# Score units and row turns placed between the v row tiles, small first-layer loads issued later: a two-layer diffusion and mixture-of-experts step

## The reference, cut to what matters

```python
def token_mixer(u, p, lam_init, rope, ctx_kv):
    proj = u @ p['w_in']
    a_in, q, k, v, c_in = jnp.split(proj, [o1, o2, o3, o4], axis=-1)
    y_pool = multiscale_pool(a_in, p['pool_w'], p['pool_scale'])
    ...
    q = apply_rope(q, cos, sin)
    k_att = jnp.concatenate([apply_rope(k, cos, sin), ctx_kv[0]], axis=1)   # latent tokens
    v_att = jnp.concatenate([v, ctx_kv[1]], axis=1)
    o = diff_attention(q, k_att, v_att, lam)       # softmax(q1 k1) - lam * softmax(q2 k2), 4 heads
    y_conv = conformer_conv(c_in, ...)             # GLU, 31 taps, LayerNorm, SiLU, pointwise
    y = jnp.concatenate([y_pool, y_attn, y_conv], axis=-1) @ p['w_out']
    return y, k, v
def trunk_layer(x, mod, p, lam_init, rope, ctx_kv):
    u = x * (1 + scale1) + shift1                  # mod = SiLU(cond) @ w_mod + b_mod
    y, k, v = token_mixer(u, p, lam_init, rope, ctx_kv)
    x = layer_norm(ALPHA * x + gate1 * y, ...)
    u = x * (1 + scale2) + shift2
    return layer_norm(ALPHA * x + gate2 * hier_moe(u, p), ...), k, v
```

## Time and profile before

| | us |
|---|---|
| median of 3 runs (1090.07 to 1093.93) | 1090.11 |
| the profiled execution | 1091.42 |
| its span in the trace | 1089.8 |
| TensorE busy with matmuls in the span | 927.5 (85%) |
| VectorE / ScalarE / POOL busy | 371.2 / 237.4 / 178.4 |

### The profile page before, as it was taken

One profiled execution on the slowest core, in us unless ns is written; L12 is line 12 of the kernel. 1 busy time (PEld: TensorE's weight loads), 2 busy tenths in 40 slices (PEclk: granted clock), 3 DMA queues, 4 the chain that ended last, 5 costly groups with the idle time before them and its releaser, 6 DMA issues.

```text
span 1089.8 us, 14815 instructions
## 1 busy us (share of the span) xinstructions
PE 927.5 (85%) x5692; PEld 551.3 (51%) x5692; DVE 371.2 (34%) x915; ACT 237.4 (22%) x568; POOL 178.4 (16%) x214
## 2 busy tenths in 40 slices
PE   5999899974999876888889998998488887778886
PEld 3655465533555534454545645553355554445444
DVE  0178452255111111112527846224611111111135
ACT  2110365042111110121220026603311111012113
POOL 5000000003222222221020000000322222222200
PEclk9999999996999999999999998999699999989998
DMA  9992261295999999997995216309699999899951
GB/s 305 373 386 115 95 251 61 87 371 203 383 413 415 413 413 413 412 392 311 380 369 215 116 46 236 125 21 376 247 354 412 414 414 413 345 415 410 414 223 58
DMA packets 80900, 321.93 MB, mean 295 GB/s; under 512 B 13359, under 2 KB 25991, under 8 KB 57537
## 3 DMA queue, kind: packets, MB, share of 16 engines
q1 hardware_dynamic: 66016, 295.72, 68.7%
q0 software_dynamic: 14816, 25.29, 6.4%
HBM read 321.46 MB, written 23.59 MB: 317 GB/s over the span
## 4 chain that ended last, share of the span: by engine, by line
PE 67%; DMA 13%; DVE 7%; SPq 6%; ACT 5%; issue 2%; POOLq 0%; ACTq 0%; DVEq 0%; POOL 0%
PE ps L1169 15%; PE ps L910 11%; DMA ring<-in_w_up 8%; PE ps L1184 8%; PE ps L1122 8%; PE ps L913 4%; PE ps L885 3%; PE ps L841 2%; DMA arena<-u_rows,row_idx 2%; PE ps L1177 2%; SPq L611 2%; SPq L604 2%; DMA ring<-in_w_mod 2%; ACT arena L1435 1%; DMA y_pairs<-tail,row_idx 1%
## 5 line engine op out<-in xcount | busy, mean ns | idle before, releaser
L1169 PE MATMUL ps<-ring,tail 128*64 128x256 f32 x1760 | 205.1, 384 | 10.2 <-DMA ring<-in_w_up 8.4
L1169 PEld LDWEIGHTS ps<-ring,tail 128*64 128x64 f32 x1760 | 144.2, 139 | 83.1 <-issue 25.2
L1908 DVE TENSOR_TENSOR arena<-arena,ps 128x128 f32<-128x128 f32 x68 | 19.5, 287 | 365.3 <-ACT arena L1470 365.3
L910 PE MATMUL ps<-uT,ring 128*128 128x384 f32 x352 | 118.2, 493 | 2.0 <-ACT uT L1319 2.0
L1184 PE MATMUL ps<-ring,krow 128*64 128x512 f32 x408 | 104.8, 633 | 3.0 <-issue 2.2
L738 POOL DMA_INDIRECT y_pairs<-tail,row_idx x58 | 57.7, 994 | 289.5 <-ACT tail L1495 283.6
L910 PEld LDWEIGHTS ps<-uT,ring 128*128 128x128 f32 x352 | 67.4, 192 | 46.2 <-issue 3.4
L1495 ACT ACTIVATE tail<-ps 128x512 f32<-128x512 f32 x58 | 34.6, 597 | 190.3 <-PE ps L1184 190.3
L733 POOL DMA_INDIRECT arena<-u_rows,row_idx x66 | 68.9, 1043 | 36.3 <-issue 20.1
L1625 DVE SCALAR_TENSOR_TENSOR arena<-arena,dw 128x414 f32<-128x414 f32 x118 | 67.6, 644 | 0.0
L1470 ACT ACTIVATE arena<-ps 128x128 f32<-128x128 f32 x68 | 18.9, 278 | 214.0 <-PE ps L1169 197.2
(11 more groups left out here) (281 smaller groups left out, 1059.8 us busy)
## 6 DMA issues: line engine op xcount, KB each, us to landing
ring<-in_w_gate SPq DMA_DIRECT2D x55, 1024.0 KB, 17.9
ring<-in_w_up SPq DMA_DIRECT2D x55, 1024.0 KB, 23.8
ring<-in_w_down SPq DMA_DIRECT2D x55, 1024.0 KB, 23.5
ring<-in_w_mod SPq DMA_DIRECT2D x10, 3072.0 KB, 10.8
arena<-in_w_gate SPq DMA_DIRECT2D x13, 1024.0 KB, 16.1
arena<-in_w_up SPq DMA_DIRECT2D x13, 1024.0 KB, 19.8
arena<-in_w_down SPq DMA_DIRECT2D x13, 1024.0 KB, 19.3
ring<-in_w_in SPq DMA_DIRECT2D x8, 1536.0 KB, 17.1
```

The lines of the kernel that those rows point to most:

```text
L910: last = mm(ps[:, n % 4, 0:T], slot[s][:, k, c:c + P], uT[:, k, :], start=(k == 0), stop=(k == KD - 1))
L1169: last = mm(ps[W * half:W * (half + 1), b, 0:2 * P].rearrange("p (j f) -> p j f", j=2), xc[:, b, k, :], gate_up_w[s][:, :, k, half * P:(ha ...
```

## The change

In layer 0, POOL waits until the fourth of the first modulation products is done before it issues the 11 small loads. On TensorE, in both layers, the key turns go between v tiles 0 and 1; the convolution turns and the scores of units 0 and 1 go between v tiles 1 and 2. For that the key turns use banks 0 and 1, and the third v tile uses bank 5. ScalarE's program follows the same order: the first v eviction, the two key copies, the second v eviction, the root, the exponentials of units 0 and 1, the third v eviction. Since `uT` is still read by the third v tile when the convolution rows are normalized, `crow` moves into the convolution accumulator and the squares' scratch `sq_out` into the GLU buffer.

```diff
-        sq_out = cacc.rearrange("p c n -> p (c n)")[:, 0:6 * VD].rearrange("p (b n) -> p b n", b=6)
+        sq_out = csil.rearrange("p c n -> p (c n)")[:, 0:6 * VD].rearrange("p (b n) -> p b n", b=6)
...
-        crow = uflat[:, 2 * T + NT * AW:2 * T + NT * AW + NT * CONV].rearrange("p (t n) -> p t n", t=NT)
+        crow = cacc.rearrange("p c n -> p (c n)")[:, 0:NT * CONV].rearrange("p (t n) -> p t n", t=NT)
...
                 pool.dma_start(dw_rows[0:TAPS, :], g["conv_dw"][l:l + 1].rearrange("o k n -> (o k) n")).then_inc(taps_loaded.sem, 16)
+                if l == 0:
+                    pool.wait_ge(mod_rows.sem, FIRST)
+                    pool.nop(nofuse=True)
                 pool.dma_start(ck_rows, g["cache_k"][0, l:l + 1].rearrange("o t h m d -> (o t) (h m d)")).then_inc(mix_loaded.sem, 16)
...
                 def project(n, s, c, rows=None, sig=proj_ready):
 
-                    if n >= 4:
+                    bank = 5 if n == 16 else n % 4
+                    if n == 16:
+                        wait(roped, l, 8)
+                    elif n >= 4:
...
-                for t in range(NT):
+                def rows_out(t):
+
                     project(14 + t, 2, 2 * P, rows=t, sig=slot_done[2] if t == NT - 1 else proj_ready)
-                    if t == 0:
-                        rotate(7)
-
-
-                wait(proj_act, l, 13)
+
+                rows_out(0)
+                rotate(7)
+                wait(proj_act, l, 12)
                 wait(mix_loaded, l, 7)
                 for h in range(HEADS):
-                    last = tr(ps[:, 2, h * P:(h + 1) * P], ck_rows[:, h * P:(h + 1) * P], ident)
+                    last = tr(ps[:, 0, h * P:(h + 1) * P], ck_rows[:, h * P:(h + 1) * P], ident)
                 last.then_inc(ck_turned.sem, 1)
-                wait(proj_act, l, 14)
                 for h in range(HEADS):
-                    last = tr(ps[:, 3, h * P:(h + 1) * P], kT[:, h, 0:SEQ], ident)
+                    last = tr(ps[:, 1, h * P:(h + 1) * P], kT[:, h, 0:SEQ], ident)
                 last.then_inc(ck_turned.sem, 1)
+                rows_out(1)
 
                 wait(conv_done, l, 1)
...
-                wait(ck_copied, l, 2)
-                wait(roped, l, 8)
...
+                wait(ck_copied, l, 2)
+                wait(roped, l, 8)
+                scores(0)
+                wait(proj_act, l, 14)
+                scores(1)
+                rows_out(2)
                 wait(proj_act, l, 15)
...
-                for u in range(NU + 3):
+                for u in range(2, NU + 3):
...
-                for t in range(NT):
+
+                def take_rows(t):
+
                     proj_wait(14 + t)
-                    fn(vrow[:, t, :], ps[:, (14 + t) % 4, 0:AW], ID).then_inc(proj_act.sem, 1)
+                    fn(vrow[:, t, :], ps[:, (2, 3, 5)[t], 0:AW], ID).then_inc(proj_act.sem, 1)
+
+                take_rows(0)
                 wait(ck_turned, l, 1)
-                fn(ckT, ps[:, 2, :].rearrange("p (h t) -> p h t", h=HEADS), ID).then_inc(ck_copied.sem, 1)
+                fn(ckT, ps[:, 0, :].rearrange("p (h t) -> p h t", h=HEADS), ID).then_inc(ck_copied.sem, 1)
                 wait(ck_turned, l, 2)
-                fn(krow[:], ps[:, 3, :], ID).then_inc(ck_copied.sem, 1)
+                fn(krow[:], ps[:, 1, :], ID).then_inc(ck_copied.sem, 1)
+                take_rows(1)
                 wait(cln_var, l, 1)
...
                         last.then_inc(scores_used.sem, 1)
+                    if u == 1:
+                        take_rows(2)
                     if u >= 3:
```

More of the change, by code:

```diff
@@ L909, in project @@
                         if rows is None:
-                            last = mm(ps[:, n % 4, 0:T], slot[s][:, k, c:c + P], uT[:, k, :],
+                            last = mm(ps[:, bank, 0:T], slot[s][:, k, c:c + P], uT[:, k, :],
                                       start=(k == 0), stop=(k == KD - 1))
                         else:
-                            last = mm(ps[:, n % 4, 0:AW], uT[:, k, rows * P:(rows + 1) * P], slot[s][:, k, c:c + AW],
+                            last = mm(ps[:, bank, 0:AW], uT[:, k, rows * P:(rows + 1) * P], slot[s][:, k, c:c + AW],
                                       start=(k == 0), stop=(k == KD - 1))
```

## The result

| | median, us | ratio to before, 95% interval |
|---|---|---|
| before (6 runs, 1090.07 to 1093.93) | 1091.15 | |
| changed (6 runs, 1080.82 to 1086.29) | 1084.51 | 0.9928 [0.9911, 0.9945] |

The change makes the kernel faster by 0.55 to 0.89%, clear of the half per cent; the medians alone differ by 6.64 us, 0.61%. One run in each of two later sets, at a far lower clock (1431.6 and 1641.83 us), is left out of the ratios. The profiled execution took 1084.30 us with a span of 1082.6, 7.2 us under that of before. Lines after the change are renumbered: L888 is the old L885, L868 the old L865, L919 the old L913, L994 the old L992, L1004 the old L1002, L844 the old L841, L1377 the old L1367. In the experiments they shift once more by a few lines; the tiles and shapes in the rows tell them apart.

A forecast was written before the change was run, and what follows sets the result against it. TensorE was taken as the bound, two thirds of the chain, DMA waits second. Terms 2.0 + 1.8 + 1.8 = 5.6 us (7.3 or 9.0 with clock held in one or both layers) off 1090.11 gave 1082.4, range 1079.5 to 1087.0.

The forecast's parts named there:

- The start: Layer 0 start: later small loads let the second modulation slice land sooner; gain 2.0 us, bounds 0 to 2.0.
- The clock: Attention's start, each layer: 1.7 us gained where full clock holds, bounds 1.0 to 2.0; leaned to at least one layer.
- rival 1: Attention's start: clock falls in both layers as before, no clock gain; 1084.5 us, chance 0.25.
- TensorE can use only the 2.01 us that it waits: Second modulation product at the start: slice up to 3.5 us sooner, but gain capped by TensorE's wait, taken 2.0.
- The price of 0 for the moved loads: q and k columns of w_in: moved loads share DMA engines, landing unchanged near 58 to 59; priced 0, range 0 to 2.
- The order: Projections to attention: turns and scores moved between v tiles bring unit 2's scores and second turn 1.8 us sooner per layer.
- The named successor of the wait: Ahead of the second turn: VectorE's maximum of unit 2, then probabilities, leave some 1.7 us idle instead of 1.15.
- half clock reaching into the modulation products: Attention's modulation products: listed as a sign that the prediction was wrong; no size given.
- rival 2: Start: gives nothing, as the second slice is late for its own length or w_in lands late; 1086.5 us, chance 0.10.
- rival 3: Projections to attention: new order gives little, through third eviction, changes of work or experts' streaming; about 1087.5 us, chance 0.13.
- rival 4: Start: slower, as moved loads hold up w_in; at 12 us late about 1096 us, chance 0.05.
- I pass the whole sum on: Later stages, experts' weight streaming included: start from TensorE signals that move up alike, so the whole sum reaches the end.

The follow-up runs named there:

- experiment 2: Changed kernel with the small loads issued as early as before, so the new order alone; ratio to before 0.9958, median 1087.86 us.
- experiment 7: Changed kernel with only the four router loads issued later, the other seven small loads as early as before; one run, 1081.71 us.
- experiment 4: Changed kernel plus unread products in TensorE's two idle stretches of each layer; ratio to before 0.9897, median 1080.48 us.
- experiment 3: Changed kernel with VectorE making unit 1's probabilities ahead of its maximum of unit 2; ratio to before 0.9891, median 1079.5 us.
- experiment 1: Kernel before with only the small loads issued later, old order of work; ratio to before 0.9964, median 1088.17 us.
- experiment 8: Kernel before, old order, plus unread products in TensorE's two idle stretches at attention's start; ratio to before 0.9984, median 1090.59 us.
- experiment 6: experiment 5 with modulation product parts in attention put two units earlier; ratio to before 0.9846, median 1075.1 us.
- experiment 5: experiment 3 with the third v eviction's wait moved from ahead of unit 2's scores to the second turn; ratio to before 0.9900, median 1081.39 us.

## Why the prediction was right, point by point

**The time.** 1084.51 us lies in the range, and 0.9928 is 0.72% against a forecast of 0.71% (1082.4 of 1090.11). That it comes so near is partly luck: two terms were off in opposite directions. The start was worth 1.9 us more than forecast, and the 2.1 us that the forecast took for the clock (7.7 less 5.6) did not come in the profile. The median is also within 0.1 us of rival 1's 1084.5, and the clock fell in both layers as rival 1 has it, so the time alone does not tell the two apart; the profile does.

**The start: mechanism right, term mis-sized.** The step that failed is the cap, "TensorE can use only the 2.01 us that it waits". A wait is the distance between two things, and one of them, TensorE's readiness at 25.77, was late by 1.7 us for half clock (5.80 us for rows that take 4.11). The landing should have been taken as the quantity, and the prediction had it right: up to 3.5 us sooner by its sum, 3.7 to 4.0 measured (27.78 to 28.09 with all loads early, 24.12 in the changed kernel). The term measured 3.9 us (2.5 to 5.4), not 2.0. The profiles bear it out: the first v tile starts at 106.29, 108.16 and 108.67 us in the three with all loads early, and at 102.24 to 105.23 in the six with all of them late. The price of 0 for the moved loads was right: the q projections start without a DMA wait at 58.23.

**The order: right.** 1.8 us a layer were forecast; 1.9 and 1.8 measured at the second turn, and the same in experiments 2 and 7; with the filling of experiment 4 the turn came 0.1 us sooner still. The details held as well: 0.69 us for the third eviction (0.7 forecast), 1.73 ahead of the second turn (1.7), cover of 3.37 us on ScalarE (3) and 3.2 us on the convolution taps (3.2). The named successor of the wait, VectorE's maximum and the probabilities behind it, was the one (experiment 3).

**The clock: mechanism right, the likeliest case wrong.** I leaned to the clock's holding in at least one layer; in the profile it fell in both, which is rival 1, and it took 0.7 us more than before from the dense product. That is also one of the prediction's own signs of being wrong, "half clock reaching into the modulation products". Counting the unfilled stretches of the new order with VectorE's program unchanged (the changed kernel, experiments 2 and 7), it held in one of six (experiment 2, layer 0), was at half for about 3.4 us in three and for 6.8 us in two; in the old order it was at half for about 6.8 us in all four (before and experiment 1). The failed step is that the rows on which I leaned compared only the stretch's work with two others; rows with the same work went both ways. One of the two, the start, stands directly behind a stretch at half clock (20.8 to 24.4 us), which the prediction's rows leave out. That the idle time of TensorE brings the fall in these stretches is shown by experiments 4 and 8, which only add work, and so is its price: 2.6 us a layer in the new order, 1.5 to 1.8 in the old. The forecast's 1.7 a layer fits the way to the first product (4.94 against 3.18 us, 1.8); the 0.7 us of the product itself was not in it. The rule of the Trainium skill quoted in the prediction ("TensorE: Matmul & The Clock Gate", "A second HAM failure mode") spoke for the fall. The profile of the changed kernel agrees with 1.64 us of work in short groups between 126.7 and 130.4 and half clock from 130.4; layer 0 of experiment 2, with the same rows and full clock, does not.

**Rivals 2, 3 and 4** fell: the start did give (experiment 1), the order's gain is whole at the second turn, and w_in is not late.

**"I pass the whole sum on": not shown in one profile.** Between the attention of either layer and the end, the profile has +1.6, +1.7 and -1.9 us where no instruction was changed. The first two and about 1.2 of the third are put down to the clock by the estimates above; the remaining 0.7 of the loss is not traced. Experiment 1 fits the passing on (3.59 us at the first v tile, 106.29 against 102.70, and 3.9 in the time), but that every term is passed on is not shown.

## What to carry to other kernels

When a wait is to be removed, price the arrival of what is waited for, not the length of the wait: the wait also depends on how late the waiting engine was, and that can be chance. When work moves under a dense stretch, read which instruction is next in each in-order queue: here a maximum stood ahead of the probabilities that were ready, and exchanging the two gave another 4 to 5 us, most of it because the clock then held. Where TensorE has idle stretches among short groups, try useful products there: in experiment 6 this brought the turns of the attention rows 1.1 us sooner in each layer than in experiment 5, and the clock held through attention.

## What the runs showed of the hardware that was not expected

- Added work made the kernel faster: with about 4 us of products that nobody reads the median was 1080.48 us in place of 1084.51 (ratios 0.9897 and 0.9928), and the granted clock stayed at 2.4 GHz from the v tiles to the modulation products.
- The same rows, to the hundredth of a microsecond, were followed by full clock in one layer and by half clock in the other (experiment 2). A fall of the clock in a profile is therefore not settled by the order of work in that stretch alone, and neither is a term that rests on one.
- Router loads of 0.14 MB in rows of 16 and 128 bytes, on another queue, delayed a 2 MB weight slice by some 1.3 to 1.6 us; 0.86 MB in longer rows delayed it by some 2.3 (one profile, experiment 7).
